# State-space groups of a two-block network: two heads' distances on ScalarE, taps ahead of mask and y tail, weight splits four slabs ahead

## What is computed

```
a_cs = jnp.cumsum(a, axis=-1)
scores = jnp.einsum('bclgn,bcsgn->bgcls', cc, bc)
mmat = scores[:, :, None] * segsum_decay(a_cs)      # exp(a_cs[l] - a_cs[s]) where s <= l, else 0
y_diag = jnp.einsum('bghcls,bcsghp->bclghp', mmat, x)
```

## Time and profile before

| | before |
|---|---|
| median of 3 runs | 1322.42 us (1321.47 to 1323.92) |
| the profiled execution | 1325.68 us, its span 1323.8 us |
| TensorE busy | 1267.2 us, 96% of the span |
| VectorE busy | 954.2 us, 72% |
| ScalarE busy | 701.4 us, 53% |
| mean granted TensorE clock | 0.966 |
| DMA | 234.66 MB, mean 177 GB/s |

### The profile page before, as it was taken

One profiled execution on the slowest core, in us unless ns is written; L12 is line 12 of the kernel. 1 busy time (PEld: TensorE's weight loads), 2 busy tenths in 40 slices (PEclk: granted clock), 3 DMA queues, 4 the chain that ended last, 5 costly groups with the idle time before them and its releaser, 6 DMA issues.

```text
span 1323.8 us, 27212 instructions
## 1 busy us (share of the span) xinstructions
PE 1267.2 (96%) x9950; PEld 1230.5 (93%) x9950; DVE 954.2 (72%) x1727; ACT 701.4 (53%) x1088; POOL 29.0 (2%) x58
## 2 busy tenths in 40 slices
PE   8989999999999999999999889889899998999997
PEld 7978999999999999999999789889899997999997
DVE  4775788888787787688888797787785555555554
ACT  4554555557346444455555656566655345444442
POOL 0000000000000000000000000000000000000000
PEclk8989999999999999999999799999999997999998
DMA  8334466675565676566655354444345553555550
GB/s 298 97 112 144 145 196 209 213 235 179 209 208 209 232 285 204 194 193 221 210 189 191 109 176 159 160 142 155 116 158 175 187 163 112 171 179 177 187 159 32
DMA packets 71567, 234.66 MB, mean 177 GB/s; under 512 B 7232, under 2 KB 15680, under 8 KB 70864
## 3 DMA queue, kind: packets, MB, share of 16 engines
q1 hardware_dynamic: 63696, 203.86, 46.6%
q0 software_dynamic: 7664, 29.92, 6.9%
q10 hardware_dynamic: 144, 0.02, 0.0%
HBM read 232.69 MB, written 1.08 MB: 177 GB/s over the span
## 4 chain that ended last, share of the span: by engine, by line
PE 52%; DVE 29%; issue 9%; ACT 8%; DVEq 1%; DMA 0%; ACTq 0%; SPq 0%; PEldq 0%
PE ps L182 15%; PE ps L183 14%; PE ps L184 14%; DVE w_lo L174 12%; DVE arena L936 3%; DVE arena L930 3%; ACT w_hi L169 2%; DVE arena L938 2%; ACT arena L879 2%; DVE arena L1637 1%; PE ps L213 1%; DVE b_lo L959 1%; DVE arena L357 1%; PE ps L1377 1%; DVE arena L955 1%
## 5 line engine op out<-in xcount | busy, mean ns | idle before, releaser
L182 PE MATMUL ps<-a_hi,w_hi 128*128 128x256 f32 x1912 | 560.7, 293 | 9.6 <-DVE a_lo L1246 5.2
L183 PE MATMUL ps<-a_lo,w_hi 128*128 128x256 f32 x1912 | 549.2, 287 | 0.0
L184 PE MATMUL ps<-a_hi,w_lo 128*128 128x256 f32 x1912 | 548.7, 287 | 0.0
L174 DVE TENSOR_TENSOR w_lo<-w_raw,w_hi 128x1024 fp32r<-128x1024 f32 x381 | 462.3, 1220 | 119.0 <-ACT w_hi L169 116.6
L182 PEld LDWEIGHTS ps<-a_hi,w_hi 128*128 128x128 f32 x1912 | 375.0, 196 | 22.3 <-issue 13.5
L169 ACT ACTIVATE w_hi<-w_raw 128x1024 fp32r<-128x1024 f32 x381 | 387.1, 1046 | 9.2 <-PE ps L184 4.7
L183 PEld LDWEIGHTS ps<-a_lo,w_hi 128*128 128x128 f32 x1912 | 375.6, 196 | 0.6 <-issue 0.2
L184 PEld LDWEIGHTS ps<-a_hi,w_lo 128*128 128x128 f32 x1912 | 375.2, 196 | 0.0
L182 PE MATMUL ps<-b_hi,w_hi 128*128 128x256 f32 x928 | 265.7, 286 | 7.3 <-DVE b_lo L959 3.5
L183 PE MATMUL ps<-b_lo,w_hi 128*128 128x256 f32 x928 | 263.4, 284 | 0.0
L184 PE MATMUL ps<-b_hi,w_lo 128*128 128x256 f32 x928 | 263.3, 284 | 0.0
(11 more groups left out here) (259 smaller groups left out, 1179.7 us busy)
## 6 DMA issues: line engine op xcount, KB each, us to landing
w_raw<-stream SPq DMA_DIRECT2D x381, 512.0 KB, 4.2
arena<-ada POOLq DMA_DIRECT2D x48, 512.0 KB, 5.4
c_hi<-cum_rows POOLq DMA_DIRECT2D x4, 1024.0 KB, 5.7
con<-consts SPq DMA_DIRECT2D x1, 1440.0 KB, 10.8
arena<-x SPq DMA_DIRECT2D x2, 512.0 KB, 4.5
out<-arena SPq DMA_DIRECT2D x2, 512.0 KB, 3.0
arena<-c_rows POOLq DMA_DIRECT2D x1, 512.0 KB, 7.3
par<-params SPq DMA_DIRECT2D x1, 301.0 KB, 11.1
```

The source lines that it names most:

```text
L174: dve.tensor_tensor(w_lo[:, s % RING], w_raw[:, s % RING], w_hi[:, s % RING].bitcast(F32), ALU.subtract).then_inc(w_lo_ready, 1)
L182: pe.matmul(o, wh, xh, start=start, stop=False, skip_group_check=shared)
L183: pe.matmul(o, wh, xl, start=False, stop=False, skip_group_check=shared)
L184: return pe.matmul(o, wl, xh, start=False, stop=stop, skip_group_check=shared)
```

## The change

The distances of heads 0 and 1 move from VectorE to ScalarE, as relu(cum[s] - cum[t]), and Exp takes them with scale -1. ScalarE starts its decays at j = 7 instead of j = 8. VectorE keeps the distances of heads 2 to 7, those of 2 and 3 at j = 7. The running sum per token is kept with its own sign. In a group the taps go ahead of the mask; the normalised y (L1602) goes from j = 5 to j = 6; ScalarE's high part of y goes behind silu(5). From j = 7 on VectorE's split stands behind x times dt, y's low part and the products. In the gates the spread of the last inverse goes from behind gate 3 to behind gate 4. All over the program ScalarE splits slab s+4 at step s; VectorE stays at s+3.

```
-                hi_ahead(act, s + 3, it, ds)
+                hi_ahead(act, s + 4, it, ds)
                 if p == 0:
                     act_inv(act, v)
-                hi_ahead(act, s + 4, it, ds)
+                hi_ahead(act, s + 5, it, ds)
                 tap(p, 0, it)
                 if p:
-                    hi_ahead(act, s + 5, it, ds)
+                    hi_ahead(act, s + 6, it, ds)
                 tap(p, 1, it)
...
                     exps(h + 1)
-                    split_hi(act, S_AOUT + 4 + h)
+                split_hi(act, S_AOUT + 4 + h)
...
-                if m == 3:
+                if m == 4:
                     tail_spread(GROUPS - 1, None)
...
+                def gaps(k):
+                    for b in range(NB):
+                        c = slice(0, SEQ) if b == 0 else slice(SEQ, SEEN)
+                        h = GROUP_HEADS * g + k
+                        h = slice(h, h + 1) if it is None else bass.ds(it * GROUP_HEADS + h, 1)
+                        act.activation(seen[k % 4][:, c], cum_all[:, k, b * P:SEQ], ACT.Relu, bias=cum_tok[:, b, h],
+                                       scale=-1.0).then_inc(first_gaps, 1)
...
+                def decays(k):
+                    if k == 0:
+                        act.wait_ge(cum_landed, in_group(16, 16, g, it))
+                    if k == 0 and not g:
+                        act.wait_ge(own_copied, 1)
+                    if k == 0:
+                        gaps(0)
+                        gaps(1)
+                    exps(k)
+                    exps(k + 1)
...
                 for j in range(GRP):
-                    if g:
+                    if g and j != 6:
                         tail(j, g - 1, it)
-                    split_hi(act, S_GRP + GRP * g + j + 3, it, GRP)
-                    if j >= 8:
-                        exps(2 * (j - 8))
-                        exps(2 * (j - 8) + 1)
+                    split_hi(act, S_GRP + GRP * g + j + 4, it, GRP)
                     if j == 6:
                         silu(5)
+                    if g and j == 6:
+                        tail(j, g - 1, it)
+                    if 7 <= j < 11:
+                        decays(2 * (j - 7))
                     used(j)
...
-                if j == 5:
+                if j == 6:
                     dve.wait_ge(inv_s_ready, in_group(1, 1, g, it))
...
-                    if k == 0:
+                    if k == 2:
                         dve.wait_ge(cum_landed, in_group(16, 16, g, it))
+                    if k == 2 and g:
+                        dve.wait_ge(yssd_ready, in_group(1, 1, g - 1, it))
...
-                    split_lo(dve, S_GRP + GRP * g + j + 3, it, GRP)
-                    if j == 5:
-                        dve.wait_ge(cb_ready, in_group(1, 1, g, it))
-                        dve.scalar_tensor_tensor(out=cb, ...
+                    if j < 7:
+                        split_lo(dve, S_GRP + GRP * g + j + 3, it, GRP)
                     if j < 6:
...
+                    if j == 5:
+                        dve.wait_ge(cb_ready, in_group(1, 1, g, it))
+                        dve.scalar_tensor_tensor(out=cb, ...
...
-                        if g:
-                            dve.wait_ge(yssd_ready, in_group(1, 1, g - 1, it))
+                    if g and j == 7:
+                        tail(j, g - 1, it)
...
-                    if 7 <= j < 11:
+                    if j in (9, 10):
                         gaps(2 * (j - 7))
                         gaps(2 * (j - 7) + 1)
+                    if j >= 7:
+                        split_lo(dve, S_GRP + GRP * g + j + 3, it, GRP)
+                    if j == 7:
+                        gaps(2)
+                        gaps(3)
...
-                    pool.wait_ge(gap_ready, 2 * GROUP_HEADS * g)
+                    pool.wait_ge(first_gaps, 4 * g)
+                    pool.wait_ge(gap_ready, 12 * g)
```

More of the change, by code:

```diff
@@ L1287, in build @@
         x_turned, x_tok_ready = sem("x_turned"), sem("x_tok_ready")
[L1288 to L1289 removed]
+        cum_stored, cum_landed, first_gaps, gap_ready, exp_done, seen_ready, y_done = (
+            sem(n) for n in ("cum_stored", "cum_landed", "first_gaps", "gap_ready", "exp_done", "seen_ready", "y_done"))
         yz_ready, ysq_ready, ysum_ready, ydiag_ready, yspread_ready, inv_s_ready = (
@@ L1620, in gaps @@
                         c = slice(0, SEQ) if b == 0 else slice(SEQ, SEEN)
-                        dve.tensor_scalar(seen[k % 4][:, c], cum_all[:, k, b * P:SEQ], neg_cum[:, b, heads_of(k)], 0.0,
-                                          ALU.add, ALU.min).then_inc(gap_ready, 1)
+                        dve.tensor_scalar(seen[k % 4][:, c], cum_all[:, k, b * P:SEQ], cum_tok[:, b, heads_of(k)], 0.0,
+                                          ALU.subtract, ALU.min).then_inc(gap_ready, 1)
                 for j in range(GRP):
-                    if g:
+                    if g and j != 7:
                         tail(j, g - 1, it)
-                    elif j in (0, 1):
+                    elif not g and j in (0, 1):
                         (softplus_series, softplus_and_cum)[j]()
-                    split_lo(dve, S_GRP + GRP * g + j + 3, it, GRP)
-                    if j == 5:
-                        dve.wait_ge(cb_ready, in_group(1, 1, g, it))
-                        dve.scalar_tensor_tensor(out=cb, in0=const("tri", SEEN), scalar=-1.0, in1=ps[:, 4, 0:SEEN],
-                                                 op0=ALU.is_gt, op1=ALU.mult).then_inc(cb_masked, 1)
+                    if j < 7:
+                        split_lo(dve, S_GRP + GRP * g + j + 3, it, GRP)
                     if j < 6:
```

40 lines of the change are left out of this document (21 added, 19 removed).

## The result

The changed kernel took 1300.25 us as the median of four executions (1300.04 to 1305.3), the kernel before 1323.17 beside it: a ratio of 0.9833, 95% interval 0.9801 to 0.9864. The same comparison made again gave 0.9875 (0.9859 to 0.989), 16.5 us (E5). Both numbers need an account, and so does the difference between them. The experiments ran on three chips: E1 to E4 on one, E5 to E8 on another, E9 to E12 on a third. Each has the kernel before beside it (1320.27, 1320.94 and 1321.07 us), so across them ratios are compared, not times.

A forecast was written before the change was run, and what follows sets the result against it. TensorE was taken as the bound, with removable waits on ScalarE and VectorE in the state-space groups. Gains of 1.7 (first group), 10.6 (three loop groups) and 1.5 us (gates) made 13.8, from 1322.42 to 1308.6 us; range 1303.5 to 1314.5.

The forecast's parts named there:

- Part 1, transposes: Before x's transposes in three loop groups: earlier silu(5) cuts the stall from 2.47 to 0.4 us; 3.56 us gained per group.
- Part 2, head 0: Before each loop group's first head: ScalarE's chain sets its start, stall 1.3 us where 1.21 was; 3.54 us per group kept.
- Part 3, first group: First state-space group: 0.5 us off the transposes' stall and head 0's 1.14 us stall gone, together 1.7 us.
- Part 4, gates: Gates: VectorE ends the pooled operand earlier, gaining 1.5 us (bounds 0 and 3.0); the spread's saved wait returns there.
- Part 4, the lead elsewhere: Outside groups and gates: VectorE's waits for w_hi lie mostly where TensorE never stops, so removing them gains nothing.
- The clock: Loop groups: one fall to half clock in each of three, 1.5 us apiece, all gone with the shorter stall.
- (a): Loop groups: TensorE still falls to half clock after the new stalls, 3 x 1.5 us lost, 1313.1 us; chance 17%.
- (b): Loop groups: ScalarE's queue becomes the bound, four relus at 2.4 us delay head 0, 1311.1 us; chance 12%.
- (d): Before the transposes: another wait was as late as the silu, so nothing moves, 1321 to 1324 us; chance 3%.
- (e): 44 feed-forward pairs: ScalarE's earlier split delays the second tap, about 0.6 us a pair, 1335.6 us; chance 3%.
- (c): Groups and gates: ScalarE and VectorE quicker, head 0 does not wait, gates' half clock goes, 1303.2 us; chance 10%.
- The forecast's last sign: Feed-forwards and MLP: their times stay unchanged to 0.1%.

The follow-up runs named there:

- E5: The changed kernel itself measured again, unaltered, on another chip: 1304.55 us, ratio 0.9875 to the kernel before.
- E1: The kernel before with only ScalarE's split moved from slab s+3 to s+4, all over the program: 1310.86 us, ratio 0.9933.
- E4: The changed kernel with the spread of the last inverse put back behind gate 3: 1306.1 us, ratio 0.9888.
- E8: The kernel before with only the new order of taps, mask and normalised y in the groups: 1325.18 us, ratio 1.0026.
- E9: The kernel before itself, unaltered, run again for a second profile: 1320.51 us, ratio 0.9991.
- E12: The changed kernel with ScalarE five slabs ahead instead of four from the first feed-forward on: 1305.28 us, ratio 0.9884.
- E10: The changed kernel with the four relus directly behind silu(5), ScalarE's j = 7 split behind two exponentials, VectorE's first products ahead of distances 2 and 3: 1300.56 us, ratio 0.9844.
- E11: The changed kernel with VectorE's splits again ahead of x times dt and the products from j = 7 on: 1309.92 us, ratio 0.9913.
- E3: The changed kernel with the distances of heads 0 and 1 back on VectorE, ScalarE's exponentials still from j = 7: 1306.23 us, ratio 0.9883.
- E2: The changed kernel with ScalarE's split back from slab s+4 to s+3 everywhere: 1312.79 us, ratio 0.9937.
- E6: The kernel before with ScalarE's split at s+4 only up to the end of the second feed-forward: 1313.49 us, ratio 0.9948.

## Why the prediction was wrong

The direction was right and the size was not. The second comparison alone would have put the time inside the range (1322.42 x 0.9875 = 1305.9 us), and that would have been luck: there the sum is 3.1 us too high in the loop groups and has nothing for 5.6 us elsewhere, and the two errors cancel in part. Point by point:

- **Part 1, transposes: right.** Idle before them 2.31 to 0.26 us, in three groups. E8 adds what the text only half said: without part 2 its time is not below that of the kernel before.
- **Part 2, head 0: right.** A stall of 1.3 was predicted, 1.2 came (873.88 less the last start at 872.55, less 0.12), and the chain through split, relus, table and Exp is the one written down. E10 and E11 moved it by about the size that the rows give, E3 by more (0.7 us, where I had 0 to 0.4). A loop group without a fall went from 47.05 to 45.0: 2.05 us, against 2.04 in the sum.
- **Part 3, first group: right in size, half right in cause.** 1.7 predicted, 2.0 came. Head 0's stall went, as predicted. The transposes' hardly moved (1.80 us idle to 1.68, where I had taken 0.5 off); it is ended by VectorE's copies (L1672), and the difference is the lead, 0.6 us (E1).
- **Part 4, gates: right in size, wrong in composition.** 1.5 predicted, 1.3 came between slabs 267 and 279. But the lead's 1.5 us, which E1 shows by itself, were spent on the later normalised y (E8), and what stayed is the spread's wait, which the text said would come back at the pooled operand and did not (E4). The half clock behind the pooled operand went in the first comparison, another 1.5, inside the bound of 3.0, but by chance: before's second trace had none to lose, and E4, E11 and E12 have it with the change's wait.
- **Part 4, the lead elsewhere: the step that failed.** "VectorE's waits for w_hi lie mostly where TensorE never stops, so they give nothing." By stages they give 1.5 us in the first feed-forward, 2.0 in the second and 2.1 at the last projection, 5.6 us that the sum had at zero; E1 and E2 show the whole by time, E6 the first two. I had read one stretch of 100 us inside a loop, where TensorE is busy 100.00, and carried it over to stage borders and loop turns. At the last projection the rows show how: in a ring of engines that is slower than TensorE by 0.17 us a slab the delay is invisible while it grows, and is paid at the end of the stage. For the 3.5 us of the feed-forwards the cause is shown to be the lead, and the way from there to TensorE stays open.
- **The clock: the other mis-sized term.** The sum took 4.5 us for three falls from one profiled execution, as if each belonged to its stall; between E9 and E5 one fall went, 1.4 us. Idle times of 2.3 us were followed by a fall three times in three in one trace of the kernel before, and once in three in the next (E9). Counted with span times one minus mean clock, which also counts idle time, the first pair of traces differs by 1323.8 x 0.034 - 1297.9 x 0.023 = 15.2 us and the second (E9, E5) by 1318.5 x 0.028 - 1302.2 x 0.026 = 3.1. The full difference of the spans is 25.9 and 16.3 us; without the clock it is 10.7 and 13.2. So of the 22.9 us of the first comparison some 6 are a matter of which executions were compared: 3.4 lie between the start and slab 26, which the change hardly touches before attention's last head.

Put together by stages, E9 against E5: loop groups 7.5, first group 2.0, gates 1.3, the lead elsewhere 5.6, and nothing net from the start, slabs 80 to 152 and the end (-1.1, 1.9, -0.8): 16.4, where the spans differ by 16.3. Rivals (a), (b), (d) and (e) did not come about. Of (c) the gates' half clock went in the first comparison, while head 0 still waits. The forecast's last sign, "the feed-forwards and the MLP unchanged to 0.1%", is the one that the profile of after refuted at once, for the feed-forwards; the MLP held (205.9 and 206.1 us).

## What to carry to other kernels

When two engines hand a tile to and fro (A waits for B's split, B's next split stands behind a wait for A), add up one turn of that ring and compare it with what TensorE needs for a slab; if it is longer, the kernel loses the difference at every tile and pays at the stage's end, and one tile more of lead on one side can open the ring. Here it cost nothing; a second one did, at one place (E12). Read the waits at stage borders and loop turns by themselves, since a busy share of 100 inside a loop says nothing about them. And before a half clock enters a sum, look at more than one execution, or compare stage by stage where the clock was whole.

## What the runs showed that I had not expected

- Whether half clock follows a stall is not settled by the stall. Behind head 0's 1.04 us of idle time it never came in the loop groups; behind 1.74 us (E3) in one of three groups, behind 2.3 us in one of three (E1, E6, E9) or three of three (before), behind 2.27 and 2.28 us at head 0 (E11, E8) in three of three. In before's kernel a fall cost a group 1.4 to 1.6 us (47.05 without, 48.45 to 48.6 with).
- The first 26 slabs took 138.6 us in one trace of the changed kernel and 142.9 in the other, which is all that differs between the two spans. Between the two of the kernel before it is 0.4 of 5.3 us, and falls further on are the rest.
- Relu on ScalarE with one operand per partition took what the nearest copy did: 1.48 us for two of 256 and two of 128 columns.
